# A two-layer hybrid decoder step on one core: first tile normed and projected alone, first weights loaded earlier, output stored in ten pieces by the sync engine

## What is computed

```python
def layer(x, w_in, w_out, norm_g, ...):
    P = rms_norm(x, norm_g) @ w_in                     # 1024 -> 4244 columns
    a, b, c, d = split(P)                              # four head groups, 256 wide each
    y = concat([mlstm(a), sparse_attention(b), rwkv7(c), memory_attention(d)])   # each times silu(z)
    return x + y @ w_out
```

## Time and profile before

| | |
|---|---|
| Time, median of three executions | 1535.96 us (1530.56, 1535.96, 1542.29) |
| Profiled execution, first to last instruction (span) | 1521.9 us |
| Own time of the profiled execution beside the span | not listed apart; the median lies 14.1 us above the span |
| PE busy | 1390.8 us, 91% |
| DVE busy / ACT busy / POOL busy | 53% / 27% / 11% |
| Mean granted clock of PE | 0.924 |
| DMA | 171.73 MB, mean 113 GB/s |

### The profile page before, as it was taken

The page is one execution under the profiler, slowest core; times in us unless marked ns, Lnnn a source line. Parts: engine busy times, 40 slices in busy tenths (PEclk is TensorE's granted clock), DMA queues, the critical chain, the costliest instruction groups (busy, mean ns, idle before and its releaser), DMA issues.

```text
span 1521.9 us, 27930 instructions
## 1 busy us (share of the span) xinstructions
PE 1390.8 (91%) x9786; PEld 990.9 (65%) x9786; DVE 810.5 (53%) x2042; ACT 406.2 (27%) x787; POOL 168.6 (11%) x312
## 2 busy tenths in 40 slices
PE   5998989998899999898999899998889999988895
PEld 2673777887875576464558467778888746755542
DVE  1355566756544845862116365575665467477610
ACT  4230101312111145651431211031111221646400
POOL 0000000000000064520000000000000002645000
PEclk9997899999779999999999879998986899999998
DMA  7231342331004155784242324224100141665701
GB/s 321 71 113 56 111 138 60 92 104 57 1 1 155 56 158 172 224 300 155 79 172 57 111 64 176 64 63 140 56 2 1 32 178 56 185 212 149 299 1 69
DMA packets 92928, 171.73 MB, mean 113 GB/s; under 512 B 14081, under 2 KB 79794, under 8 KB 86898
## 3 DMA queue, kind: packets, MB, share of 16 engines
q1 hardware_dynamic: 79778, 120.39, 23.9%
q0 software_dynamic: 13008, 49.54, 9.5%
HBM read 157.08 MB, written 21.12 MB: 117 GB/s over the span
## 4 chain that ended last, share of the span: by engine, by line
PE 71%; DVE 15%; issue 8%; ACT 3%; DMA 1%; SPq 0%; POOL 0%; DVEq 0%; POOLq 0%; ACTq 0%
PE bank L581 16%; PE bank L618 12%; PE bank L1188 8%; PE bank L2801 4%; PE bank L514 2%; PE bank L1214 2%; PE bank L814 2%; PE bank L1322 2%; PE bank L1310 1%; DVE area L1680 1%; DVE area L1715 1%; PE bank L822 1%; PE bank L800 1%; PE bank L584 1%; PE bank L1299 1%
## 5 line engine op out<-in xcount | busy, mean ns | idle before, releaser
L581 PE MATMUL bank<-stream,hT 128*128 128x512 f32 (+3 forms) x768 | 261.6, 497 | 0.5 <-DVE hT L451 0.5
L618 PE MATMUL bank<-hT,stream 128*128 128x272 f32 x960 | 225.8, 396 | 5.6 <-DVE area L1558 5.4
L618 PEld LDWEIGHTS bank<-hT,stream 128*128 128x128 f32 x960 | 182.3, 191 | 44.4 <-DVE area L1558 6.0
L581 PEld LDWEIGHTS bank<-stream,hT 128*128 128x128 f32 x768 | 145.9, 194 | 100.2 <-issue 86.5
L1188 PE MATMUL bank<-stream,prm 128*128 128x256 f32 x512 | 126.3, 409 | 0.4 <-DVE YT L1539 0.4
L2801 PE MATMUL bank<-stream,YT 128*128 128x512 f32 x256 | 114.3, 609 | 4.8 <-DVE YT L2709 4.8
L1188 PEld LDWEIGHTS bank<-stream,prm 128*128 128x128 f32 x512 | 104.8, 207 | 18.0 <-issue 1.4
L2801 PEld LDWEIGHTS bank<-stream,YT 128*128 128x128 f32 x256 | 49.5, 195 | 67.2 <-issue 61.9
L407 POOL DMA_DIRECT2D stream<-in_slcK x128 | 69.0, 549 | 169.2 <-PE bank L584 135.5
L407 POOL DMA_DIRECT2D stream<-in_slcV x128 | 68.5, 539 | 72.3 <-PE bank L2253 30.0
L2817 DVE TENSOR_TENSOR X<-bank,X 128x512 f32<-128x512 f32 x16 | 11.1, 692 | 102.4 <-PE bank L2801 102.4
(11 more groups left out here) (634 smaller groups left out, 2286.6 us busy)
## 6 DMA issues: line engine op xcount, KB each, us to landing
stream<-in_cmpL SPq DMA_DIRECT2D x256, 128.0 KB, 2.3
stream<-in_win_ SPq DMA_DIRECT2D x12, 2048.0 KB, 7.6
stream<-in_slcK SPq DMA_DIRECT2D x128, 64.0 KB, 2.3
stream<-in_slcK POOLq DMA_DIRECT2D x128, 64.0 KB, 2.5
stream<-in_slcV SPq DMA_DIRECT2D x128, 64.0 KB, 2.8
stream<-in_slcV POOLq DMA_DIRECT2D x128, 64.0 KB, 2.8
stream<-in_wout SPq DMA_DIRECT2D x4, 2048.0 KB, 11.0
out_winpast<-in_winraw POOLq DMA_DIRECT2D x2, 4064.0 KB, 26.6
```

Of the source, the lines that this page charges most:

```text
L581: last = nc.tensor.matmul(ps[:, 0:w], hT[:, k, tok(i)], ws[:, k, :], start=(k == 0), stop=(k == KT - 1))
L618: last = nc.tensor.matmul(ps[:, 0:HALF], ws[:, k, 128 * f:128 * f + 128], hT[:, k, HALF * s:HALF * s + HALF], start=(k == 0), stop=(k == K ...
```

## The change

1. **Constants in two parts.** `misc` moves from the end of `cst` to just behind the identity. The first 136 columns (68 KB, semaphore `consth`) are loaded where the whole was; the other 1162 KB (`const`) later.
2. **Order of the first loads.** `x` tile 0, head of constants, gains, `T0`, and then tiles 1 to 4 of `x`, the page table, the rest of the constants, `F0`, `prm0`, `T1`. `pe_norm` and `act_norm` wait for the head; `pe_m` and `dve_m` wait for the rest.
3. **First tile by itself.** In layer 0 `act_norm` runs in the groups (0) and (1, 2, 3, 4): square, Ln, Exp and scaling of tile 0 before the squares of the others. The columns of sums are renumbered.
4. **PE's order in layer 0.** Turn 0, project 0, turn 1, project 1, turn 2, project 2, turn 3 and 4, project 3, project 4. In layer 1 it stays one tile ahead.
5. **The final store.** SP, after its last load, waits for each addition of `dve_out` in turn and stores that tile's half, ten DMAs of 256 KB, and waits for their landing. POOL no longer stores `y`; it waits for the state stores alone.

```diff
@@ sync_stream(sp)
             for it in items:
+                if it == ("w", 0, "F0"):
+                    for i in range(1, TILES):
+                        sp.dma(f"xt{i}", sp.eng.dma_start(X[:, i, :], io["x"][:, i, :]).then_inc(x_in[i], 16), "xt", i)
+                    sp.dma("ptab", sp.eng.dma_start(ptab[:, :], io["ptab"]).then_inc(ptab_in, 16), "ptab")
+                    sp.dma("const", sp.eng.dma_start(cst[:, NHEAD:], io["const"][:, NHEAD:]).then_inc(const_in, 16), "const")
@@ act_norm(act, l)
+            def col(i):
+                return (i + 1) % 5 if l else i + 1
             if l:
                 barrier(act, ("N", l - 1))
-            first = (0, 1, 2, 3, 4) if l == 0 else (4, 0, 1, 2)
-            for group in (first, (3,)) if l else (first,):
+            for group in ((4, 0, 1, 2), (3,)) if l else ((0,), (1, 2, 3, 4)):
...
-                act.wait_ge(const_in, at("const"))
-                c = slice(0, 5) if l == 0 else slice(0, 4) if len(group) > 1 else slice(4, 5)
+                act.wait_ge(head_in, at("consth"))
+                c = slice(group[0] + 1, group[-1] + 2) if l == 0 else slice(0, 4) if len(group) > 1 else slice(4, 5)
@@ pe_norm(pe, l)
-            pe.wait_ge(const_in, at("const"))
+            pe.wait_ge(head_in, at("consth"))
             pe.wait_ge(sem_of_slot("w", l, "T0"), at("here", "w", l, "T0"))
             order = norm_order(l)
+            ahead = (0, 1, 2, 4, 4) if l == 0 else (1, 2, 3, 4, 4)
+            turned = 0
             pe_norm_tile(pe, l, order[0])
             for k, i in enumerate(order):
-                if k + 1 < TILES:
-                    pe_norm_tile(pe, l, order[k + 1])
-                    if k + 2 == TILES:
+                while turned < ahead[k]:
+                    turned += 1
+                    pe_norm_tile(pe, l, order[turned])
+                    if turned + 1 == TILES:
                         phase_end(pe, "E", l)
@@ pe_m, dve_m
+            pe.wait_ge(const_in, at("const"))
...
+            dve.wait_ge(const_in, at("const"))
@@ dve_out(dve, l)
+                    dve.name("xo", l + 1, hf, i)
@@ block.sync
-            sp.dma("const", sp.eng.dma_start(cst[:, :], io["const"]).then_inc(const_in, 16), "const")
+            sp.dma("consth", sp.eng.dma_start(cst[:, 0:NHEAD], io["const"][:, 0:NHEAD]).then_inc(head_in, 16), "consth")
             sp.dma("prmg0", sp.eng.dma_start(prm[:, 0:16], io["prm"][0, :, 0:16]).then_inc(gains_in[0], 16), "prmg", 0)
-            for i in range(1, TILES):
-                sp.dma(f"xt{i}", sp.eng.dma_start(X[:, i, :], io["x"][:, i, :]).then_inc(x_in[i], 16), "xt", i)
-            sp.dma("ptab", sp.eng.dma_start(ptab[:, :], io["ptab"]).then_inc(ptab_in, 16), "ptab")
             sync_stream(sp)
+            for hf in range(2):
+                for i in OUT_ORDER[hf]:
+                    sp.wait_ge(dve_done, at("xo", DEPTH, hf, i))
+                    c = slice(512 * hf, 512 * hf + 512)
+                    sp.dma("st_end", sp.eng.dma_start(io["y"][:, i, c], X[:, i, c]).then_inc(y_stored, 16), "end")
+            sp.wait_ge(y_stored, at("end"))
@@ block.gpsimd
-            pool.wait_ge(dve_done, at("x", DEPTH))
-            pool.dma("st_end", pool.eng.dma_start(io["y"], X).then_inc(y_stored, 16), "end")
-            pool.wait_ge(y_stored, at("end"))
```

More of the change, by code:

```diff
@@ L82, in constants @@
     c["idn"] = np.eye(128)
+    m = np.zeros((128, 8))
+    m[:, 0], m[:, 1], m[:, 2], m[:, 3] = EPS, 1.0, RW_EPS, 10 * np.log(2.0)
+    c["misc"] = m
     c["onesbd"] = (p[:, None] // 64 == t[None] // 64)
@@ L140 @@
 CONST, COFF = constants()
+NHEAD = 136
 PARAMS = [("g", 8), ("mg", 8), ("cw", 16), ("cb", 4), ("gb", 8), ("mlg", 256), ("qkg", 512), ("kcg", 1),
@@ L257, in build @@
         plan.banks = [ctx.enter_context(nc.psum_tensor(f"bank{i}", [128, 512], F32)) for i in range(8)]
-        names = ["pe", "dve", "act", "pool", "const", "prm0", "prm1", "prmg0", "prmg1", "memx0", "memx1", "ptab",
+        names = ["pe", "dve", "act", "pool", "consth", "const", "prm0", "prm1", "prmg0", "prmg1", "memx0", "memx1", "ptab",
                  "st_end"] + [f"slot{i}" for i in range(NSLOT)] + [f"page{i}" for i in range(NSLOT)]
@@ L268, in build @@
         done = {n: plan.sems[n] for n in ("pe", "dve", "act", "pool")}
-        const_in, ptab_in, y_stored = (plan.sems[n] for n in ("const", "ptab", "st_end"))
+        head_in, const_in, ptab_in, y_stored = (plan.sems[n] for n in ("consth", "const", "ptab", "st_end"))
         x_in = [plan.sems[f"xt{i}"] for i in range(TILES)]
@@ L434, in act_norm @@
                         act.wait_ge(x_in[i], at("xt", i))
-                    act(nc.scalar.activation(E["junk"], X[:, i, :], ACT.Square, accum_out=E["ss"][:, (i + 1) % 5:(i + 1) % 5 + 1]).then_inc(act_done, 1))
-                act.wait_ge(const_in, at("const"))
-                c = slice(0, 5) if l == 0 else slice(0, 4) if len(group) > 1 else slice(4, 5)
+                    act(nc.scalar.activation(E["junk"], X[:, i, :], ACT.Square, accum_out=E["ss"][:, col(i):col(i) + 1]).then_inc(act_done, 1))
+                act.wait_ge(head_in, at("consth"))
+                c = slice(group[0] + 1, group[-1] + 2) if l == 0 else slice(0, 4) if len(group) > 1 else slice(4, 5)
                 act(nc.scalar.activation(E["rs"][:, c], E["ss"][:, c], ACT.Ln, bias=eps, scale=1.0 / D).then_inc(act_done, 1))
@@ L440, in act_norm @@
                 for i in (i for i in norm_order(l) if i in group):
-                    act(nc.scalar.mul(E["xn"][i], X[:, i, :], E["rs"][:, (i + 1) % 5:(i + 1) % 5 + 1]).then_inc(act_done, 1), "xn", l, i)
+                    act(nc.scalar.mul(E["xn"][i], X[:, i, :], E["rs"][:, col(i):col(i) + 1]).then_inc(act_done, 1), "xn", l, i)
             act.name("xnall", l)
@@ L2788, in build @@
         POOL_STAGES = (pool_m, pool_r, pool_n,)
+        OUT_ORDER = ((0, 1, 2, 3, 4), (4, 0, 1, 2, 3))
         def pe_out(pe, l):
@@ L2796, in pe_out @@
                 w = slot("wout", l, hf).rearrange("p (k c) -> p k c", k=KT)
-                for i in ((0, 1, 2, 3, 4), (4, 0, 1, 2, 3))[hf]:
+                for i in OUT_ORDER[hf]:
                     ps = pe.open("out", l, hf, i)
```

3 lines of the change are left out of this document (removed).

## The result

The changed kernel takes 1519.82 us (median of 17 executions, 1509.09 to 1526.71); the kernel before, 17 executions beside it, 1530.56. The ratio is 0.9918 with a 95% interval of 0.9893 to 0.9942: faster by 0.8%, 12.6 us of 1531, between 8.9 and 16.4; the two medians themselves are 10.7 us apart. Each ratio in this document compares only executions within 1.5% of the fastest one of their kernel on that chip, the medians take all. The profiled execution has a span of 1511.8 us, 10.1 less than before.

A forecast was written before the change was run, and what follows sets the result against it. PE was taken as the bound, with time to gain only at its two ends: span 1521.9 less 3.1 in front and 13.0 behind is 1505.8, plus 14.1 from span to median gives about 1520 us, range 1512 to 1529.

The forecast's parts named there:

- What bounds the kernel: Whole kernel: PE, busy 91% of 1521.9 us, is the bound; 18.7 us in front and 16.6 behind have PE idle.
- The end, 13.0 us: After the last addition: 4.8 us less store and 8.2 us of POOL's DRAIN hidden; gain 13.0 us, 11.8 to 13.7.
- The front, 3.1 us: Start up to F0: F0 begins at 50.9 instead of 53.95, a gain of 3.1 us, 1.6 to 4.6.
- the line of the landings: First loads: DMA queue serves in order at 2.43 us for each 1000 KB, so T0 lands at 10.05.
- if `T0` lands after 12: First loads: one of the stated signs that the prediction is wrong; T0 was forecast to land at 10.05.
- My upper bound of 3.0 for the clock: PE's start: 3 us more work at half rate in the first projection would lose 3.0 us; 1.5 was taken.
- ACT's cover: Layer 0 norm: xn of tile 1 comes at 20.5 while PE is in its first projection, so its cost is hidden.
- The sum: Whole kernel: span 1521.9 - 3.1 - 13.0 = 1505.8, plus 14.1 us of median above span, gives 1519.9, say 1520.
- Rival (a): Program's end: POOL's DRAIN of 8.16 us stays on the path after SP's landing; gain 7.9, time 1528; chance 10%.
- (b): First loads: the queue shares, T0 and tiles land near 15.0, front loses 4.4 us; time 1524.3; chance 9%.
- (c): T0 stage: PE's clock stays low through the new pauses, 27.9 us more, time 1548; chance 4%.
- (d): Final store: the ten pieces do not come early, waits answered late or pieces queue; 1525 at worst; chance 2%.

The follow-up runs named there:

- the single store on SP: Changed kernel, but SP stores the whole of X in one DMA after the last addition, instead of ten pieces; 7.9 us from last addition to end.
- the warm run: Changed kernel, but PE turns the identity 40 times into an unread bank until T0 lands; F0 begins at 52.30 us.
- four small edits: Changed kernel plus 40 warm turns, T0 in four DMAs, norm groups (0), (1, 2), (3, 4), tiles 1 and 2 turned together; median 1510.17 us, ratio 0.9873.

## Why the prediction was right, and where not

- **What bounds the kernel**: right. PE is the bound, time was to be had before its first and after its last instruction, and the middle moved as one, as far as its spread of 5 us can tell.
- **The end, 13.0 us**: 14.1. The DRAIN went off the path as worked out (8.7 us by the single store on SP, 8.2 forecast). The last piece landed in 2.0 us, below the lower bound of 2.3 that I had from a load of half its size; this term was mis-sized by 1.0, and with it the gain lies above my 11.8 to 13.7. The Trainium skill ("VectorE: DVE Perf Modes", section on the DRAIN you can't avoid) has 12 ns for the closing DRAINs; ACT's 8 ns and DVE's 17 come near it, but POOL's took 8160 to 12303 ns and PE's 7915 in every trace here. PE's ends 0.05 us after its last matmul, so it covers work and costs nothing. The estimate by the fit in the Trainium skill ("DMA: Bandwidth & Descriptors", anatomy of one DMA), 2.6 us for the piece, is nearer to the 2.0 measured than my 3.0; the fit is for GpSimd's path, and there the piece took 2.3.
- **The front, 3.1 us**: 0.3 in the profile after, 1.0 by the mean of five profiles with this front (`F0` at 53.36 in the mean) and two of the old one (53.88 and 54.82), 0.6 to 2.1 by the line through all executions. The step that failed is the landing of `T0`: 10.05 by the line of the landings, 12.6 measured, 11.5 to 12.6 over the profiles, and "if `T0` lands after 12" was one of my own signs of being wrong. All of the 2.1 us by which PE started late went through to `F0`. The first projection came to 8.82 us where I had 6.87 + 1.5, 0.45 more: the low level cost 1.7 (8.82 less 7.13), near my 1.5, and a projection behind a pause takes 7.13 where I had 6.87. My upper bound of 3.0 for the clock misread the row: before, 2.9 us went by at the low level, which cost half of that. The pauses of PE were 1.14, 1.14 and 0.54 us where I had 1.3 each; that hid the longer projections, and from one tile to the next it took 9.15 us where I had 9.07.
- **ACT's cover**: "PE will be in its first projection until later" held in the changed kernel by a microsecond, since the low clock made that projection long. In the warm run the cover was gone and the wait of 1.27 us was there.
- **The sum**: the 14.1 us between span and median were taken for something outside the program. They are not: an execution's time is its span plus 1.6 or 1.7 us in each of the 120. The rest was that the profiled execution of the kernel before had drawn a mean clock of 0.924 where its executions have 0.915 on average. The wrong reading cancelled in the difference, and the base of 1536 turned out as 1530.56, which covered for a gain 3.5 us smaller than forecast (12.6 by the ratio). That the forecast met the median is luck to this extent.
- **Rival (a)**, the DRAIN stays: refuted by its place at 1438.1 and by the single store. **(b)**, the queue shares: the landing was late as it said, half of the way to it, but sharing is not the main reason; alone in the queue `T0` was no earlier than 11.4. **(c)**, the clock stays low: it stayed low up to 18.9 us, the fourth matmul of the first projection, and rose. **(d)**: nine of the ten pieces landed in 2.0 us and one in 3.1, and none held up the last.

## What to carry to other kernels

Look at each engine's closing instructions before you give the end of a program to a store: an engine whose own last work lies early can have its closing cost hidden, and here that was worth more (8.7 us) than the shorter store (5.5). When a start is pulled forward, follow it stage by stage to the next point where all tiles meet; of these six microseconds nearly all were lost to a cold first projection and bare hand-overs between tiles, and four small edits there brought six back. A load moved to the front of the queue need not keep the rate that it had further back: here it was 2.6 us late. Before comparing medians, put the time against the granted clock of each execution.

## What was not expected of the hardware

- POOL's DRAIN at the end takes 8.2 us behind a landed store of 2560 KB and 8.9 behind landed pieces of 256 KB. Begun while POOL's reload was in flight it takes 10.4 to 12.3 us and ends 4.06 us after the landing, in 11 of 11 traces.
- Packets of 16 KB took 611 to 621 ns in the kernel before, from 11.6 us on, but up to 1744 ns (727 on average) for those of `T0` in the profile after, which began between 3.9 and 11.7 us. Those of the constants in the kernel before, 9840 bytes from 3.5 us on, took 369 to 468 ns, at full rate.
- A store of 256 KB from SP lands in 2.0 us, from POOL in 2.3.
- Executions of one program lie up to 2.3% apart (1514.53 to 1549.31 for the kernel before on one chip), and nearly all of it goes with the time spent at PE's low clock: 14.3 us for each 0.01 of mean clock.
